# One core, two model blocks in exact-split matrix products: the second block's first norm on raw rows turned half by half, with the rows' factors applied by VectorE at the projections' exits

## What is computed

```python
h_res = jnp.concatenate([meta, x], axis=1)              # 16 + 256 = 272 rows
h = rmsnorm_2(h_res, g_mix_pre[l])                      # the norm that is changed
proj = h @ w_in[l]
u_a, c_g, b_g, v_b, gate_logits = jnp.split(proj, splits, axis=-1)
y_a = fourier_mix(u_a) @ w_fourier[l]
conv_in = c_g * v_b
y_b = (b_g * centred_dwconv(conv_in, conv_w_mix[l], conv_b_mix[l])) @ w_conv_out[l]
gates = jax.nn.sigmoid((gate_logits + b_gates[l]).reshape(bn, L, N_BRANCHES, D_MODEL))
merged = gates[:, :, 0] * y_a + gates[:, :, 1] * y_b
```

## Time and profile before

| | |
|---|---|
| Time, median of 3 runs | 1001.74 us (999.83 to 1002.95) |
| The profiled execution: its own time | 1001.64 us |
| The profiled execution: span from first to last instruction | 999.8 us |
| PE busy | 981.8 us of the span (98%) |
| DVE / ACT / POOL busy | 593.9 / 530.5 / 351.7 us |
| TensorE clock granted, mean | 0.997 of full speed |
| HBM | 168 GB/s over the span |

### The profile page before, as it was taken

How to read it: one execution, slowest core, us unless ns; L and a number is a source line. 1 busy time by engine, 2 the same in 40 slices (tenths; PEclk the granted TensorE clock), 3 DMA queues, 4 the chain that set the end, 5 groups by cost and what they waited for, 6 DMA issues and landing times.

```text
span 999.8 us, 15057 instructions
## 1 busy us (share of the span) xinstructions
PE 981.8 (98%) x6330; PEld 887.3 (89%) x6330; DVE 593.9 (59%) x806; ACT 530.5 (53%) x720; POOL 351.7 (35%) x109
## 2 busy tenths in 40 slices
PE   9999999999999999899999999999999999999997
PEld 7888889999888888779999888799999999999885
DVE  4997946888321535426888312446218589888643
ACT  6676346555333566546555333545543687666532
POOL 0021045665656553345565666364640000000000
PEclk9999999999999999999999999999999999999999
DMA  9453224544555452424554555354444425555541
GB/s 335 169 197 137 85 102 159 198 175 176 204 194 185 169 205 90 167 92 166 188 191 168 205 177 208 140 173 165 169 169 168 169 106 211 176 197 176 191 146 42
DMA packets 24807, 168.51 MB, mean 169 GB/s; under 512 B 2781, under 2 KB 3092, under 8 KB 4900
## 3 DMA queue, kind: packets, MB, share of 16 engines
q1 hardware_dynamic: 24452, 167.22, 46.7%
q10 hardware_dynamic: 288, 0.33, 0.1%
HBM read 166.49 MB, written 1.05 MB: 168 GB/s over the span
## 4 chain that ended last, share of the span: by engine, by line
PE 90%; DVE 4%; ACT 3%; issue 1%; DMA 1%; SPq 0%; DVEq 0%; ACTq 0%
PE bank L641 28%; PE bank L643 27%; PE bank L642 27%; PE bank L841 2%; ACT whi L1142 1%; DVE wlo L1704 1%; DMA raw<-w_stream 1%; PE bank L669 1%; PE bank L809 0%; PE bank L858 0%; PE bank L934 0%; PE bank L1050 0%; PE bank L1034 0%; PE bank L877 0%; PE bank L951 0%
## 5 line engine op out<-in xcount | busy, mean ns | idle before, releaser
L2345 POOL TENSOR_TENSOR wlo<-raw,whi 128x1024 fp32r<-128x1024 f32 (+1 forms) x102 | 350.6, 3439 | 382.1 <-ACT whi L1142 374.5
L1704 DVE TENSOR_TENSOR wlo<-raw,whi 128x1024 fp32r<-128x1024 f32 (+2 forms) x152 | 246.7, 1623 | 305.2 <-ACT whi L1142 305.2
L1142 ACT ACTIVATE whi<-raw 128x2048 fp32r<-128x2048 f32 (+1 forms) x154 | 292.8, 1902 | 151.1 <-PE bank L643 149.1
L641 PE MATMUL bank<-nhi,whi 128*128 128x256 f32 (+3 forms) x832 | 238.2, 286 | 1.2 <-DVE nlo L1712 1.2
L642 PE MATMUL bank<-nlo,whi 128*128 128x256 f32 (+3 forms) x832 | 235.5, 283 | 0.0
L643 PE MATMUL bank<-nhi,wlo 128*128 128x256 f32 (+3 forms) x832 | 235.0, 283 | 0.0
L641 PEld LDWEIGHTS bank<-nhi,whi 128*128 128x128 f32 (+1 forms) x832 | 158.2, 190 | 4.8 <-issue 4.7
L642 PEld LDWEIGHTS bank<-nlo,whi 128*128 128x128 f32 (+1 forms) x832 | 158.3, 190 | 0.1
L643 PEld LDWEIGHTS bank<-nhi,wlo 128*128 128x128 f32 (+1 forms) x832 | 158.3, 190 | 0.0
L641 PE MATMUL bank<-mhi,whi 128*128 128x258 f32 x384 | 109.3, 285 | 1.7 <-DVE mlo L2179 1.0
L643 PE MATMUL bank<-mhi,wlo 128*128 128x258 f32 x384 | 108.4, 282 | 0.0
(11 more groups left out here) (292 smaller groups left out, 1568.6 us busy)
## 6 DMA issues: line engine op xcount, KB each, us to landing
raw<-w_stream SPq DMA_DIRECT2D x154, 1024.0 KB, 4.8
cst<-consts SPq DMA_DIRECT2D x1, 1200.0 KB, 11.7
h<-x_rows SPq DMA_DIRECT2D x4, 256.0 KB, 5.4
raw<-w_stream SPq DMA_DIRECT2D x2, 512.0 KB, 6.4
out_rows<-e SPq DMA_DIRECT2D x4, 256.0 KB, 2.0
e<-g_post SPq DMA_DIRECT2D x1, 512.0 KB, 3.6
raw<-w_stream SPq DMA_DIRECT2D x1, 352.0 KB, 9.5
b<-consts_x SPq DMA_DIRECT2D x1, 272.0 KB
```

Of the source, the lines that this page charges most:

```text
L641: pe.matmul(out, lhsT.hi, rhs.hi, start=start, stop=False)
L1142: act.activation(whi[j][:, 0:n], raw[j][:, 0:n], ACT.Copy).then_inc(s_hi.up(i))
L1704: dve.tensor_tensor(wlo[j][:, 0:m], raw[j][:, 0:m], whi[j][:, 0:m].bitcast(F32), ALU.subtract).then_inc(s_lod.up(i))
L2345: pool.tensor_tensor(wlo[j][:, m:n], raw[j][:, m:n], whi[j][:, m:n].bitcast(F32), ALU.subtract).then_inc(s_lop.up(i))
```

## The change

What it does, in order of the program:

- The last product of the first block turns the first half of the raw `h` inside its last tile, as the other three do, and DVE evacuates it ahead of its last addition. The second half is turned after the first quarter of the first input tile, whose two blocks `u` 0 and `u` 1 are now made together in four quarters. The 32 transposes L987 and L994 give way to 16 (`half_turn`), and the squares' chain and DVE's two multiplications by 1/rms go.
- ACT makes the factors with `row_stats(4)` and copies the turned raw banks into `HT` behind it; these banks now serve both the norm and the residual.
- To apply the factors, they are needed along the free axis on all partitions: DVE makes four 128x128 diagonal matrices (1/rms and its square, two row tiles each), PE multiplies them by a matrix of ones (two matmuls of 256 columns, the bank `rowf4`), and ACT copies the two results to `RSB2` (1/rms) and `RS2` (1/rms squared).
- DVE applies them: `u` and `gt` are evacuated by DVE with `RSB2`, `cg` with `RS2` (which serves `cg` times `cv`), and `bg` gets a second multiplication. ACT no longer evacuates `u` and `cg`, and its sigmoid now works in place behind DVE.
- ACT does `hi` of tiles IN2+2 and IN2+3 after all this, and DVE does `lo` of them between its exits of `u`.

```diff
@@ tensor program
-            out_tok(3, DOWN[1], 16, lambda k: FF[1][:, k, :], lambda k: [s_fflo.at(1, k // 2)], None, (0, 2, 1, 3))
-            for q in range(4):
-                u = begin("res", q)
...
-            us = [begin("nT", q) for q in range(4)]
-            for tt in range(2):
-                on.wait_ge(*s_xnt.at(tt))
...
+            out_tok(3, DOWN[1], 16, lambda k: FF[1][:, k, :], lambda k: [s_fflo.at(1, k // 2)], None, (0, 2, 1, 3),
+                    lambda: half_turn(4, 0))
...
-            blocks("u", IN2, 4, 0)
+            us = [begin("u", m) for m in range(2)]
+            w = weights(IN2, 8)
+            weights_in(IN2)
+            for n in range(4):
+                m = n % 2
+                for k in range(n // 2 * 4, n // 2 * 4 + 4):
+                    on.wait_ge(*n_ready(4, k))
+                    x = mm3(us[m].t[:, 0:L2], w[:, k, m * P:m * P + P], nT2[:, k, :], k == 0, k == 7)
+                if n >= 2:
+                    x.then_inc(us[m].full)
+                if n == 0:
+                    half_turn(4, 1)
+            u = begin("rowf4")
+            on.wait_ge(*TC)
+            on.wait_ge(*s_dg4.at(1))
+            for j in range(2):
+                x = pe.matmul(u.t[:, j * 256:j * 256 + 256], ones, DG4[:, j * 256:j * 256 + 256], start=True, stop=True)
+            x.then_inc(u.full)
+            for m in range(2, 4):
+                feat(weights(IN2 + 1, 8), IN2 + 1, begin("u", m), m % 2 * P, 0, lambda k: n_ready(4, k))
@@ scalar program
-                act.activation(xn[:, tt, :], h[:, tt, :], ACT.Square, accum_out=small[:, tt:tt + 1]).then_inc(own.up())
-                on.wait_ge(*own.last())
-                inv_rms(small[:, tt:tt + 1], small[:, 2 + tt:3 + tt], D, s_nrs.up(tt))
...
+            for c in range(2):
+                half_turn(4, c)
+            row_stats(4)
             for q in range(4):
-                u = use["res", q]
-                on.wait_ge(*u.done())
+                u = use["tr", 4, q]
+                on.wait_ge(*s_nodd.at(q))
                 act.activation(HT[:, 2 * q:2 * q + 2, META:L2], u.t[:, :].rearrange("p (k t) -> p k t", k=2), ACT.Copy).then_inc(u.free)
...
-                act.activation(UT[:, m, :], u.t[:, 0:L2], ACT.Copy).then_inc(u.free)
+            u = use["rowf4",]
+            on.wait_ge(*u.done())
+            on.wait_ge(*s_one.at(0))
+            act.activation(RSB2[:, META:L2], u.t[:, 0:256], ACT.Copy)
+            act.activation(RS2[:, 2:N2], u.t[:, 256:512], ACT.Copy).then_inc(u.free)
+            hi(IN2 + 2)
+            hi(IN2 + 3)
...
-                act.activation(GT[:, g, :], u.t[:, 0:N2], ACT.Sigmoid, bias=vcol("b_gates", g)).then_inc(u.free)
+                on.wait_ge(*use["gt", g].gone())
+                act.activation(GT[:, g, :], GT[:, g, :], ACT.Sigmoid, bias=vcol("b_gates", g)).then_inc(s_gate.up(g))
@@ vector program
-            out_h(3, 3, None)
-            for tt in range(2):
-                on.wait_ge(*s_nrs.at(tt))
-                dve.tensor_scalar(xn[:, tt, :], h[:, tt, :], small[:, 2 + tt:3 + tt], None, ALU.mult).then_inc(s_xnt.up(tt))
...
+            out_h(3, 3, 4)
+            half_turn(4, 1)
+            dve.memset(RSB2[:, 0:META], 1.0)
+            dve.memset(RS2[:, 0:2], 1.0).then_inc(s_one.up(0))
+            for j in range(2):
+                on.wait_ge(*s_stat.at(4, 1 + j))
+                for tt in range(2):
+                    x = dve.tensor_scalar(DG4[:, j * 256 + tt * P:j * 256 + tt * P + P], ident, stats[4][2 + j][:, tt:tt + 1], None, ALU.mult)
+                x.then_inc(s_dg4.up(j))
+            def scaled(dst, u, r):
+                on.wait_ge(*use["rowf4",].gone())
+                on.wait_ge(*u.done())
+                dve.tensor_tensor(dst, u.t[:, 0:r.shape[1]], r, ALU.mult).then_inc(u.free)
             for m in range(4):
-                if m % 2 == 0:
-                    lo(IN2 + m // 2 + 2)
+                scaled(UT[:, m, :], use["u", m], RSB2)
+                if m % 2:
+                    lo(IN2 + 2 + m // 2)
...
                 dve.tensor_tensor(CV[:, m, :], CV[:, m, :], u.t[:, 0:N2], ALU.mult).then_inc(u.free)
+                on.wait_ge(*u.gone())
+                dve.tensor_tensor(CV[:, m, :], CV[:, m, :], RSB2[:, X0:L2], ALU.mult).then_inc(s_bgr.up(m))
...
+                scaled(GT[:, g, :], use["gt", g], RSB2[:, X0:L2])
```

More of the change, by code:

```diff
@@ L354, in plan_banks @@
     banks.take("metaT")
-    out(3, DOWN[1], 16)
-    for q in range(4):
[L357 to L362, removed]
+    out(3, DOWN[1], 16, (), 4)
+    for m in range(2):
+        banks.take("u", m, hold=True)
+    banks.take("tr", 4, 2)
+    banks.take("tr", 4, 3)
+    for m in range(2):
+        banks.drop("u", m)
+    banks.take("rowf4")
+    for m in range(2, 4):
+        banks.take("u", m)
+    for i in range(2):
+        last[IN2 + i] = (("u", 2 * i + 1), 0)
     banks.take("resm")
@@ L447, in block_kernel @@
         small = sb("small", 256)
-        rows = sb("rows", 32)
+        rows = sb("rows", 40)
         room = place[0]
@@ L485, in block_kernel @@
         GAIN = ["g_mix0", "g_ffn0", "g_mix1", "g_ffn1", "g_mix_pre"]
-        stats = [[rows[:, 8 * t + 2 * i:8 * t + 2 * i + 2] for i in range(4)] for t in range(4)]
+        stats = [[rows[:, 8 * t + 2 * i:8 * t + 2 * i + 2] for i in range(4)] for t in range(5)]
         A = Area("a")
@@ L609, in block_kernel @@
         s_mr, s_mn, s_mhi, s_mlo = (sig(n, [0]) for n in ("mr", "mn", "mhi", "mlo"))
-        s_nrs, s_xnt = sig("nrs", range(2)), sig("xnt", range(2))
+        s_bgr, s_dg4, s_one, s_nodd, s_gate = sig("bgr", range(4)), sig("dg4", range(2)), sig("one", [0]), sig("nodd", range(4)), sig("gate", range(16))
         s_cvid, s_ybhi, s_yblo, s_fthi = (sig(n, range(4)) for n in ("cvid", "ybhi", "yblo", "fthi"))
@@ L621, in n_ready @@
         def n_ready(t, k):
-            return (use["tr", t, k // 2] if t < 4 else use["nT", k // 2]).gone() if k % 2 else s_nlo.at(t, k // 2)
+            if k % 2 == 0:
+                return s_nlo.at(t, k // 2)
+            return use["tr", t, k // 2].gone() if t < 4 else s_nodd.at(k // 2)
         def h_ready(t):
@@ L1533, in scalar_program @@
             act.activation(HT[:, :, 0:META], u.t[:, 0:P].rearrange("p (k t) -> p k t", k=8), ACT.Copy).then_inc(u.free)
-            for m in range(4):
-                if m % 2 == 0:
-                    hi(IN2 + 2 + m // 2 + 2)
-                u = use["cg", m]
-                on.wait_ge(*u.done())
-                act.activation(CG[:, m, :], u.t[:, 0:N2], ACT.Copy).then_inc(u.free)
+            hi(IN2 + 4)
+            hi(IN2 + 5)
             for m in range(4):
@@ L2142, in vector_program @@
             dve.tensor_copy(EO[:, :, 0:1], UT[:, :, 0:1]).then_inc(s_eo0.up(0))
+            for m in range(4):
+                if m % 2 == 0:
+                    lo(IN2 + 4 + m // 2)
+                scaled(CG[:, m, :], use["cg", m], RS2)
             for m in range(4):
@@ L2184, in vector_program @@
                     u = use["ya", m]
-                    on.wait_ge(*use["gt", m].gone())
+                    on.wait_ge(*s_gate.at(m))
                     on.wait_ge(*u.done())
```

60 lines of the change are left out of this document (17 added, 43 removed).

## The result

The changed kernel takes 1008.76 us (median of 4 runs, 1008.07 to 1009.96) against 1001.63 (median of 4 runs, 999.83 to 1002.95): a ratio of 1.0072, with a 95% interval of 1.0055 to 1.0089. It is slower, and lies 7.9 us above the upper end of the forecast's range. The profiled execution took 1008.07 us with a span of 1006.2, so the two profiled executions differ by 6.4 us, and it is these 6.4 that the traces can explain.

What follows compares the result with a forecast made beforehand. PE, busy 98% of the span, was taken as the bound, so only its waits or superfluous work could be saved. The boundary's 2.6 us off 1001.64, with exits at nothing, gave 999.0 us; range 997.6 to 1000.9.

Steps and rivals of the forecast that it cites:

- The boundary: From the last product's end to `cg`: 19.36 us before, with `cg` to start 2.6 us earlier after the change.
- `u`'s first matmul to the last factor: At the boundary: the last factor done 6.90 us behind `u`'s first matmul, from 6.81 at t = 3 plus 0.09.
- the wait of the ones-matmuls: At the boundary: PE waits 0.75 us for DVE's diagonals before the ones-matmuls; bounds nothing and 1.3 us.
- The weights of `cg`: Before `cg`: tile ready 653.3, PE asks 653.53, 0.2 us cover; rival says late, gain 1.6, 1000.1 us, chance 0.2.
- So I cost the exits at nothing; their cover is that bank reserve of over 10 us: 28 exits of `u`, `cg`, `bg`, `gt` add 0.42 us each on DVE, hidden since banks are needed five or six blocks later.
- about 0.4 us later per pair of blocks, against a cover of several microseconds: In the gates: the sigmoid behind DVE delays ACT's `hi` by this much, taken as covered.
- The second multiplication of `bg`: In `bg`: POOL's subtraction may lengthen it by up to 2.2 us, at most 4.4 in all, without changing the total.
- the exits become the path: Rival, from `cg` to the last gate: 24 blocks each hold PE 0.42 us, 10.1 in all; 1009 us, chance 0.06.
- The forecast's base: Whole kernel: the profiled 1001.64 us, from which only the boundary's 2.6 us was subtracted.

Runs made afterwards that it cites:

- before_rows40: Kernel before with only the buffer `rows` grown from 32 to 40 columns, no instruction differing: 1005.11 us, ratio 1.0041.
- change_rows48: Changed kernel with 48 columns in `rows` instead of 40: 1003.55 us, ratio 1.0028 to the kernel before.
- change_rows64: Changed kernel with 64 columns in `rows` instead of 40, a shift of 128 bytes against the kernel before: 1007.36 us in one run.
- before_rows48: Kernel before with 48 columns in `rows` instead of 32, a shift of 64 bytes: 999.02 us, ratio 0.9971.
- all_mended: Changed kernel with `dc` 0 copies before the table load, even gates' exits before `lo`, `bg`'s factor applied to `cv` early, `rows` of 48: 996.54 us, ratio 0.996.

## Why the prediction was wrong, step by step

- **The boundary** (gain 2.6 us) was right: 19.36 us became 16.61, a gain of 2.75, though all of it stood 1.6 us later. `u`'s first matmul to the last factor took 6.84 us where 6.90 was forecast; the wait of the ones-matmuls was 0.52 instead of 0.75; `cg` came 15.41 us behind `u` and was forecast at 15.46. It is this stretch alone that the earlier trace rows were read for.
- **The weights of `cg`** (rival of chance 0.2) were in time. ACT's tile began at 649.11, 9.42 us behind `u`'s start, where 9.5 was forecast, and `cg` followed the residual's transposes without a wait.
- **"So I cost the exits at nothing; their cover is that bank reserve of over 10 us"** is the step that failed. For the banks it was true: no bank exit held PE, in any of the kernels. But an exit was also put ahead of ACT's next instructions, and one of them, the copies of `dc` 0, had 0.6 us of cover. The prediction named the sigmoid behind DVE, costed it at "about 0.4 us later per pair of blocks, against a cover of several microseconds", and was wrong in both numbers. The delay was 1.7 us, since the exit stands behind DVE's 1.2 us `lo`, which itself waits for ACT's `hi`; and the cover was that of weight tiles, not of the Fourier part. One look at what ACT does behind sigmoid 0 and at PE's start of `dp` 0 would have shown it.
- **The second multiplication of `bg`** was costed in length (up to 2.2 us longer, measured 1.7, of which 1.3 had stood elsewhere on the same path before) and wrongly held hidden because "the product of `bg` is wanted only after the 16 gates". The product is, but ACT's copy of it stands ahead of the table load and of everything behind that. It made 1.8 of the 3.66 us.
- **The rival "the exits become the path"** named the right line ("ACT's sigmoid and the Fourier part hang behind it in order") with a price in the wrong form: 0.42 us at each of 24 blocks instead of one overrun of 3.7 us, whose wait cost nearly as much again in clock in the profiled execution. It had a chance of 0.06 because DVE's free half was held against it; busy shares say nothing of an order.
- **What was not costed at all**: the 8 more elements of `rows`. They made 3.3 of the 8 us of loss in the first two down products, and 0.25 more in the second block's, at places where the program is unchanged, and the prediction has no term for them. before_rows40 has them by itself: its span is 3.5 us longer than that of the kernel before. The forecast's base, that all outside the boundary takes what it took, is the second step that failed.

With these: 1001.64 - 2.75 + 3.3 (places) + 3.8 (wait) + 3.1 (clock) + 0.5 (end) - 1.7 (the first block) = 1007.9, against the profiled 1008.07.

## What to carry to other kernels

An instruction that moves to another engine brings its queue along: cost not its duration but the whole distance in order, what stands ahead of it on the new engine and what stands behind the waiter on the old, up to the next instruction that PE needs, and read that instruction's own cover (its end against PE's start) instead of a busy share. Where two engines now wait for each other in turns (`hi`, `lo`, exit, sigmoid), put what PE needs next ahead of the turn. And when an allocation grows, compare the spacing of matmuls in a stretch that the change doesn't touch before explaining anything; a control that has the new places and the old program costs one line.

## What the runs showed of the hardware

- The spacing of the same 128x512 matmuls at full clock, fed without any wait, depended on where their stationary operand lies relative to buffers that stay: 0.2292 us in the kernel before, 0.2336 with 32 or 128 bytes more, 0.2270 with 64; in the second block's down product 0.2324, and 0.2334, 0.2289 and 0.2269 with 32, 64 and 128. For the first two down products together this is up to 4.8 us of 1000. A shift of everything by 32 bytes changed nothing. The Trainium skill, page "SBUF — State Buffer", section "Who interferes with whom", says that only the port pair shared by VectorE and GpSimd causes contention and that PE never waits; these runs show a dependence of PE on its operands' places that this rule doesn't cover, and its cause stays open.
- A short wait of PE can cost twice. After 3.7 us without a matmul the granted clock fell to 0.50 and 3.1 us more were lost in the changed kernel, 3.2 in change_rows48 and 1.6 in change_rows64; after 1.9 us it fell in one kernel (1.6 us lost) and not in another; after 1.15 us it stayed. After the three waits of the old boundary, 2.3 us in all, it fell in one profiled execution of an otherwise faster kernel (before_rows48, 1.55 us lost) and stayed in the others. The wait of 2.9 us in the first block, the same in every kernel, was followed by the full clock in the profiled execution of the changed kernel and by 0.83 on average over 400 to 410 in those of the kernel before and of all_mended, which is the 1.7 us in the last row of the table.
